# Expert loop of a mixture-of-experts stage: the two SwiGLU halves placed one weight tile earlier in the orders of VectorE and ScalarE

## The reference

```python
hb = x_pad[toks] @ w1[e] + b1[e]                      # 1024 -> 2048
g_part = jnp.minimum(hb[..., ::2], SWIGLU_LIMIT)      # even columns
u_part = jnp.clip(hb[..., 1::2], -SWIGLU_LIMIT, SWIGLU_LIMIT)   # odd columns
act = g_part * jax.nn.sigmoid(SWIGLU_ALPHA * g_part) * (u_part + 1)
return act @ w2[e] + b2[e]                            # 1024 -> 1024
```

## Time and profile before

| | |
|---|---|
| three runs | 4045.22, 4045.79, 4039.15 us; median 4045.22 |
| the profiled execution | 4038.55 us, of which the span of its instructions is 4036.8 |
| busy share of the span | TensorE 89%, VectorE 60%, ScalarE 43%, GpSimd 12% |
| mean granted clock of TensorE | 0.916 of full speed |
| weights of the expert loop | 768 transfers of 512 KB |

### The profile page before, as it was taken

One profiled execution on the slowest core, in us unless ns is written; L12 is line 12 of the kernel. 1 busy time (PEld: TensorE's weight loads), 2 busy tenths in 40 slices (PEclk: granted clock), 3 DMA queues, 4 the chain that ended last, 5 costly groups with the idle time before them and its releaser, 6 DMA issues.

```text
span 4036.8 us, 43749 instructions
## 1 busy us (share of the span) xinstructions
PE 3572.9 (89%) x13692; PEld 2488.9 (62%) x13692; DVE 2408.2 (60%) x2911; ACT 1725.4 (43%) x2321; POOL 503.4 (12%) x623
## 2 busy tenths in 40 slices
PE   7978899999987899997886689959999999999996
PEld 3437468874446478875544454437777777777774
DVE  5333365556243375553337762048888889898895
ACT  2134142322143142233220112027778777877773
POOL 0000000000000000000000000014343434343440
PEclk9975899999966899997997789969999999999998
DMA  4202223331211223330110002239999999999994
GB/s 173 69 26 69 62 74 95 96 96 63 63 53 47 63 84 94 94 99 26 42 45 3 1 0 78 78 115 336 331 349 334 356 332 353 339 345 343 341 354 174
DMA packets 167552, 615.18 MB, mean 152 GB/s; under 512 B 18480, under 2 KB 18608, under 8 KB 166992
## 3 DMA queue, kind: packets, MB, share of 16 engines
q1 hardware_dynamic: 156768, 573.84, 40.3%
q0 software_dynamic: 10672, 39.85, 3.6%
HBM read 586.35 MB, written 27.26 MB: 152 GB/s over the span
## 4 chain that ended last, share of the span: by engine, by line
PE 64%; DVE 14%; DMA 8%; ACT 7%; issue 6%; POOL 0%; DVEq 0%; SPq 0%; ACTq 0%; POOLq 0%
PE bank L560 52%; PE bank L1023 9%; DMA sb_ring<-in_w 6%; DVE w_part L2257 2%; ACT w_part L1486 2%; DVE sb_rstd L1580 2%; DVE sb_work L2284 1%; DVE sb_work L2288 1%; DVE sb_work L2279 1%; PE bank L1031 1%; DVE sb_work L2281 1%; PE bank L992 1%; ACT sb_work L1194 0%; DVE sb_work L2019 0%; ACT sb_work L1223 0%
## 5 line engine op out<-in xcount | busy, mean ns | idle before, releaser
L2257 DVE TENSOR_TENSOR w_part<-sb_ring,w_part 128x1024 fp32r<-128x1024 f32 x762 | 893.5, 1223 | 125.9 <-ACT w_part L1486 125.5
L1486 ACT ACTIVATE w_part<-sb_ring 128x1024 fp32r<-128x1024 f32 x762 | 772.2, 1053 | 141.9 <-PE bank L1023 79.4
L1023 PE MATMUL bank<-w_part,xg_hi 128*128 128x512 f32 x2048 | 566.1, 398 | 0.0
L560 PE MATMUL bank<-h_hi,split_part 128*128 128x512 f32 x1408 | 443.4, 400 | 8.3 <-ACT h_hi L1293 8.3
L1023 PEld LDWEIGHTS bank<-w_part,xg_hi 128*128 128x128 f32 x2048 | 384.7, 189 | 89.7
L560 PE MATMUL bank<-sb_work,sb_ring 128*128 128x512 f32 (+4 forms) x864 | 333.1, 541 | 22.2 <-DVE sb_modv L1570 10.5
L1023 PE MATMUL bank<-w_part,xg_lo 128*128 128x512 f32 x1024 | 322.1, 396 | 0.0
L560 PEld LDWEIGHTS bank<-h_hi,split_part 128*128 128x128 f32 x1408 | 267.4, 190 | 74.9 <-issue 8.4
L560 PE MATMUL bank<-sb_work 128*128 128x64 f32 (+6 forms) x992 | 257.3, 466 | 48.7 <-DVE sb_work L1789 22.8
L1023 PE MATMUL bank<-w_part,act_hi 128*128 128x512 f32 x1024 | 284.6, 399 | 0.1
L560 PEld LDWEIGHTS bank<-sb_work,sb_ring 128*128 128x128 f32 (+3 forms) x864 | 163.4, 190 | 187.3 <-issue 158.2
(11 more groups left out here) (323 smaller groups left out, 4996.4 us busy)
## 6 DMA issues: line engine op xcount, KB each, us to landing
sb_ring<-in_w SPq DMA_DIRECT2D x768, 512.0 KB, 7.1
sb_ring<-in_wstream SPq DMA_DIRECT2D x304, 512.0 KB, 3.5
y_rows<-sb_padc POOLq DMA_DIRECT2D x1, 4096.0 KB, 27.2
sb_xT<-in_x SPq DMA_DIRECT2D x1, 2048.0 KB, 11.4
x_rows<-sb_padc SPq DMA_DIRECT2D x1, 2048.0 KB, 22.5
x_rows<-sb_work SPq DMA_DIRECT2D x1, 2048.0 KB, 12.7
sb_work<-y_rows SPq DMA_DIRECT2D x4, 512.0 KB, 5.2
out_h<-sb_xT SPq DMA_DIRECT2D x1, 2048.0 KB, 6.3
```

The costliest lines, as they stand in the source:

```text
L560: ins = nc.tensor.matmul(out, l, r, start=start, stop=stop)
L1023: ins = nc.tensor.matmul(out[n][:], l[:, k, :], r[:, n * 512:(n + 1) * 512], start=False, stop=(k, p) == (KD - 1, 2))
L1486: nc.scalar.activation(w_hi[t % SPLITS], ring[:, t % RING, :], ACT.Copy).then_inc(s_hi, 1)
L2257: nc.vector.tensor_tensor(w_lo[t % SPLITS], ring[:, t % RING, :], w_hi[t % SPLITS].bitcast(F32), ALU.subtract).then_inc(s_lo, 1)
```

## The change

`swiglu` and `sigmoid` of both halves stand one tile further ahead: behind tile 12 instead of 13, and behind tile 20 instead of 21. The copy of `meta` on ScalarE moves with `sigmoid(0)`. `round_act`, `rest_of_act` and TensorE's order stay where they are: act rounding of half 0 behind tile 15, of half 1 behind tile 23 on ScalarE and behind tile 22 on VectorE. No instruction is added or taken away.

```diff
 # ScalarE
-                for t in range(SPLITS, KD + SPLITS):
+                for t in range(SPLITS, KD + SPLITS - 1):
                     round_tile(i, t)
                 sigmoid(0)
                 if more:
                     ...   (meta copy)
-                for t in range(KD + SPLITS, KD + SPLITS + 2):
+                for t in range(KD + SPLITS - 1, KD + SPLITS + 2):
                     round_tile(i, t)
                 round_act(0)
-                for t in range(KD + SPLITS + 2, 2 * KD + SPLITS):
+                for t in range(KD + SPLITS + 2, 2 * KD + SPLITS - 1):
                     round_tile(i, t)
                 sigmoid(1)
-                for t in range(2 * KD + SPLITS, MOE_TILES):
+                for t in range(2 * KD + SPLITS - 1, MOE_TILES):
                     round_tile(i, t)
                 round_act(1)
 # VectorE
-                for t in range(SPLITS, KD + SPLITS):
+                for t in range(SPLITS, KD + SPLITS - 1):
                     rest_of_tile(i, t)
                 swiglu(0)
-                for t in range(KD + SPLITS, KD + SPLITS + 2):
+                for t in range(KD + SPLITS - 1, KD + SPLITS + 2):
                     rest_of_tile(i, t)
                 rest_of_act(0)
-                for t in range(KD + SPLITS + 2, 2 * KD + SPLITS):
+                for t in range(KD + SPLITS + 2, 2 * KD + SPLITS - 1):
                     rest_of_tile(i, t)
                 swiglu(1)
-                rest_of_tile(i, 2 * KD + SPLITS)
+                for t in range(2 * KD + SPLITS - 1, 2 * KD + SPLITS + 1):
+                    rest_of_tile(i, t)
                 rest_of_act(1)
```

## The result

The changed kernel takes 3970.98 us in the median of five runs (3967.48 to 3975.80) against 4045.22 us (4036.06 to 4045.83). The ratio is 0.9825, 95% interval 0.9811 to 0.9839: 74 us faster, where 3979 was forecast. So the gain is 1.75 to 2.0%.

A forecast was written before the change was run, and what follows sets the result against it. TensorE and DMA were both candidates in the expert loop. Waits of 2.61 us a block less 0.3 and DMA's 0.35 gave 1.95 x 32 = 62 us: 3976 or 3983 by starting point, called 3979; range 3950 to 4022.

The forecast's parts named there:

- The step that made the wait: VectorE's g_part of half 0 queues behind tile 13, whose late transfer it does not need; TensorE waits 1.58 us a block.
- Rival 2: The wait only moves: tile 13's transfer delays tile 13's product instead of g_part; no gain, 4045 us; chance 0.06.
- Half 0: TensorE's wait before its transposes at L1031 goes: 1.58 us a block, plus 0.21 for the pipeline start.
- Half 1: TensorE's second wait at L1031, 0.54 us, goes too; gain 0.82 us a block, hanging on tile 20's transfer.
- given back: Before tile 20: half 1's activation late, since ScalarE rounds three tiles first; costs 0.3 us a block.
- DMA's 0.35 us a block: In the expert loop, DMA was taken to cost 0.35 us a block over TensorE's own 37.45 us.
- The bound of 39.0 us: Upper DMA bound on a block: 13.6 MB at 349 GB/s, the busiest stretch found; the low bound was 36.5 us.
- Rival 1: DMA becomes the expert loop's bound at 38.3 to 39.0 us a block: 3999 to 4021 us; chance 0.22.
- The sum: Expert-loop block: 39.75 us less 2.61 of waits, plus 0.3 and 0.35 of costs, gives 37.8; gain 62 us.
- The rule of the Trainium skill: HBM transfers bound at about 358 GB/s per core: 38.0 us a block, gain some 56 us instead of 62.
- Rival 3: Ring slots released some 0.85 us later delay tile 21 and next block's tile 5: adds 26 us, 4071; chance 0.07.
- rival 4: More than forecast: all 95.1 us of the weight loads' wait at L1031 are won, 3950 us; chance 0.05.

The follow-up runs named there:

- half 0 alone: Kernel before, with only half 0's swiglu and sigmoid (and the copy of meta) moved one tile ahead: 3985.67 us, ratio 0.9871.
- half 1 alone: Kernel before, with only half 1's swiglu and sigmoid moved one tile ahead: 4012.08 us, ratio 0.9927.
- half1_two: Changed kernel with half 1's swiglu and sigmoid one more tile ahead, behind tile 19: 3970.20 us, ratio 0.9824.

## Why the prediction was right, by its steps

- **The step that made the wait.** Right, and shown: taking away the cause of tile 13's lateness gives 57 us with the old order (51 of them in the loop), and moving half 0 past tile 13 gives 53. Rival 2 (the wait only moves) is out as a whole; in part it is real, see half 0 alone.
- **Half 0.** The prediction's 1.58 + 0.21 = 1.79 us a block are 57 us; alone it measures 53, from which half 1's later start has already taken 0.23 us a block, some 7 us.
- **Half 1.** The prediction's 0.82 less 0.3 are 16.6 us; alone it measures 26, which is the 0.82 with nothing given back. The term that was mis-sized is the 0.3 "given back" for the act rounding behind three tiles. With half 1 alone it measures nothing: tile 20 starts late in no block. In the whole change it is there, but smaller: in 16 of 31 blocks tile 20 starts a tenth of a microsecond or more late, 0.35 at the most, 0.17 on average. In the block shown it is 0.35, and L2294 of half 1 ends at 3009.17, 0.13 us before tile 20's 3009.30:

```profile
3008.49 0.68 DVE L2294 TENSOR_TENSOR act_lo<-bank,act_hi 128x512 fp32r<-128x512 f32 x1
```

  Each late tile 20 stands 0.12 to 0.13 us behind the end of an L2294, so the mechanism was right. One tile further (half1_two) it is 0.62 us.
- **DMA's 0.35 us a block.** Mis-sized too. What is left at L1031 is 5.1 us in the matmul records, 0.16 a block, and by late starts 0.08 + 0.18 = 0.26. Without the accumulating write it is 0.01, so it hangs on transfers as forecast. The bound of 39.0 us, from the stretch with 0.99 and 349 GB/s in the earlier trace rows, was wrong in kind: the changed kernel moves 362 GB/s over the whole loop, and up to 369 GB/s over a block at a share of 1.00. A share of 0.99 did not mean that no more bytes could flow. Rival 1 did not come.
- **The sum.** 37.8 us a block forecast, 37.53 measured; 62 us forecast, 71 in the two profiled executions (4036.8 - 3965.7) and 74 in the medians. TensorE's floor without any wait or give-back is 39.75 - 2.61 = 37.14 in the prediction, and measured 37.06. On top of it the prediction put 0.3 and 0.35, 0.65 us a block; the changed kernel has 0.47, of which late starts explain 0.17 and 0.26. So the forecast came true by its own mechanism, with both costs too high.
- **The rule of the Trainium skill.** By the estimate from its 358 GB/s a block would take 38.0 us. The block takes 37.53, the loop ran at 362 GB/s on average and single blocks at up to 369, so this trace does not agree with that figure as a limit here. The Trainium skill itself, on its page DMA: Bandwidth & Descriptors, in the section Measured, ties the figure to both cores of a pair streaming and gives 425 GB/s for one alone with transfers of 16 MB. No run here had a second core at work.
- **What was to be seen.** g_part directly behind tile 12, the wait at L1031 under 10 us in the matmul records (not in the weight loads', 13.3), over 355 GB/s: seen. That it would be almost all half 1's was not: half 0 starts late in 6 blocks, half 1 in 12. L2288's first and last start 60 us closer: 68.3. A new wait for L2294: one recorded case, and the late starts of tile 20.
- **Rival 3 and rival 4.** Tiles 13 and 21 are not late for TensorE: at L1023 it waits for nothing but the small cases named and, in the weight loads' records, once for L2257 (1.3 us, in the last block). Rival 4's 95 us were not all won; 13.3 of them are still there, and tile 20 is new.

The range held, and the result lies between the forecast and its lower end. I had given DMA too much of the uncertainty.

## What to carry to other kernels

In an engine's written-out order, put a step that others wait for in front of work that it does not need, above all work with a transfer behind it: here two steps moved past one tile each gave 1.75 to 2.0%. Then work the next meeting point of the engines again with the new times, since a wait removed at one place can come back at the next where the other engine has no gap (a wait of 0.54 us became 1.38 in some blocks, and with only one engine's order changed in nearly all). Stop when the bound engine is busy throughout; further moves gave nothing.

## What the hardware showed that I had not expected

- The accumulating indirect write of the result rows (512 KB, from GpSimd's queue), issued beside the weight loads, costs the old order 57 us, 51 in the loop of 32 blocks and 6 behind it. The changed order pays only 13 to 23 us for the same write, the 6 behind the loop among them. Whether the accumulation or the bytes do it was not tried.
- A DMA share of 0.99 to 1.00 stood beside 349 GB/s before and 355 to 369 after, each over about a block. It did not tell how near DMA was to its end.
- TensorE's matmuls can start late without a wait in their records: in the block shown tile 20 starts 0.35 us late and the matmul records have no idle time there. The distances between starts show it, and so do the weight loads' records (0.34 us, put down to no engine).
